# Output projections and mix of a two-layer block as three fp32r passes, with a share of the elementwise work on GpSimd

## The reference, cut to what matters

```python
y_a = nsa_attention(...) @ w_attn_o[l]          # (512, 512) @ (512, 1024)
y_b = spatial_gating(...) @ w_sgu_o[l]          # (512, 256) @ (256, 1024)
y_c = s5_layer(...) @ w_s5_o[l]                 # (512, 256) @ (256, 1024)
g_a, g_b, g_c = jnp.split(jax.nn.sigmoid(branch_g), 3, axis=-1)
merged = g_a * y_a + g_b * y_b + g_c * y_c
x = x + merged @ w_mix_o[l]                     # (512, 1024) @ (1024, 1024)
h = rms_norm(x, norm_ffn_g[l])
x = x + hierarchical_moe(h, ...)                # 32 experts, 6.3 MB of weights each
```

## Time and profile before

| | |
|---|---|
| median of 3 runs | 1970.93 us (1968.88 to 1974.15) |
| the profiled execution, its own time | 1967.01 us |
| its span in the trace | 1965.3 us |
| mean granted clock of TensorE | 0.989 |
| PE busy | 1899.9 us (97%) |
| DVE, ACT, POOL busy | 945.9, 431.4, 99.4 us |

### The profile page before, as it was taken

How to read it: one execution, slowest core, us unless ns; L and a number is a source line. 1 busy time by engine, 2 the same in 40 slices (tenths; PEclk the granted TensorE clock), 3 DMA queues, 4 the chain that set the end, 5 groups by cost and what they waited for, 6 DMA issues and landing times. The chain is left out here.

```text
span 1965.3 us, 26006 instructions
## 1 busy us (share of the span) xinstructions
PE 1899.9 (97%) x10104; PEld 1122.1 (57%) x10105; DVE 945.9 (48%) x1875; ACT 431.4 (22%) x816; POOL 99.4 (5%) x205
## 2 busy tenths in 40 slices
PE   6999999999999999999899999999999999999995
PEld 4868777645554454454357877775465455455442
DVE  7754555345443443443478455553363343343344
ACT  4413444102211111111233244440121111111112
POOL 4500000000000000000063000000000000000000
PEclk9999999999999999999999999999999999999998
DMA  4222112333699999999722221132528999999993
GB/s 165 65 92 86 65 63 67 129 107 157 266 425 426 425 429 426 425 426 426 321 70 65 92 73 68 54 105 89 216 91 338 426 427 423 428 430 422 423 428 156
DMA packets 56398, 482.10 MB, mean 245 GB/s; under 512 B 9584, under 2 KB 22384, under 8 KB 27376
## 3 DMA queue, kind: packets, MB, share of 16 engines
q1 hardware_dynamic: 56304, 480.80, 60.4%
HBM read 476.59 MB, written 4.19 MB: 245 GB/s over the span
## 5 line engine op out<-in xcount | busy, mean ns | idle before, releaser
L1756 DVE TENSOR_TENSOR x_tokens<-x_tokens,ps 128x512 f32<-128x512 f32 x240 | 161.7, 687 | 236.9 <-PE ps L990 236.0
L1056 PE MATMUL ps<-arena,branch 128*64 128x512 f32 x512 | 226.6, 595 | 0.0
L1056 PE MATMUL ps<-slabs,branch 128*64 128x512 f32 x512 | 226.6, 595 | 0.0
L1006 PE MATMUL ps<-slabs,arena 128*64 128x512 f32 x512 | 225.0, 592 | 0.7 <-issue 0.7
L1006 PE MATMUL ps<-arena 128*64 128x512 f32 x512 | 225.0, 592 | 0.1
L1007 PE MATMUL ps<-arena 128*64 128x512 f32 x512 | 225.1, 592 | 0.0
L1007 PE MATMUL ps<-slabs,arena 128*64 128x512 f32 x512 | 225.0, 592 | 0.0
L749 PE MATMUL ps<-h_hi,w_parts 128*128 128x512 f32 x768 | 210.8, 408 | 1.5 <-DVE w_parts L1411 1.5
L749 PEld LDWEIGHTS ps<-h_hi,w_parts 128*128 128x128 f32 x768 | 135.1, 189 | 38.8 <-issue 9.2
L1006 PEld LDWEIGHTS ps<-slabs,arena 128*64 128x64 f32 x512 | 70.1, 137 | 146.0 <-issue 145.9
L1006 PEld LDWEIGHTS ps<-arena 128*64 128x64 f32 x512 | 70.0, 137 | 144.8 <-issue 144.8
(11 more groups left out here) (346 smaller groups left out, 2972.5 us busy)
## 6 DMA issues: line engine op xcount, KB each, us to landing
arena<-in_expert_w_gate SPq DMA_DIRECT2D x32, 2048.0 KB, 12.4
arena<-in_expert_w_up SPq DMA_DIRECT2D x32, 2048.0 KB, 16.8
arena<-in_expert_w_down SPq DMA_DIRECT2D x32, 2048.0 KB, 9.8
slabs<-in_expert_w_gate SPq DMA_DIRECT2D x32, 2048.0 KB, 15.4
slabs<-in_expert_w_up SPq DMA_DIRECT2D x32, 2048.0 KB, 19.9
slabs<-in_expert_w_down SPq DMA_DIRECT2D x32, 2048.0 KB, 14.1
slabs<-in_gate_w SPq DMA_DIRECT2D x24, 1024.0 KB, 4.8
slabs<-in_dense SPq DMA_DIRECT2D x10, 2048.0 KB, 8.1
```

What stands on the lines that cost most here:

```text
L1006: nc.tensor.matmul(ps[0:64, BANK_GU[b], :], xk, low[:, k, :], start=(k == 0), stop=(k == ND - 1), tile_position=(0, 0))
L1056: done = nc.tensor.matmul(ps[64 * b:64 * b + 64, BANK_Y[half], :], hidT[:, k, CAP * b:CAP * (b + 1)], w_down[b][:, k, half * 512:(half + 1 ...
L1756: v.tensor_tensor(xs, xs, ps[:, BANK_BACK[n % 2], :], ALU.add).then_inc(s["back_added"], 1)
```

## The change

The output projections and the mix become three fp32r passes. The three branch outputs, the merged rows and the four kinds of weights are each split in a high and a low part. The two weight slabs of the output projections become four half slabs (k = 20 to 23), the two of the mix four (k = 24 to 26, and a fourth, here called 27, that goes to the gates' place). PE makes 24 separate products p (`OUT_PRODUCTS`: branches 1, 2, 0 for columns 0 to 3, then for 4 to 7) into six rotating banks; DVE merges each by one instruction (`outp_free`), GpSimd adds the first two branches (`sum_two`), and DVE adds the third. The low parts of the mix weights are made by GpSimd as well. Of the first expert weights only one slab is loaded at `merge_done` 8 instead of four. The core of the diff:

```diff
-N_SLAB = 24
+N_SLAB = 28
-S_KS, S_V, S_CMP, S_GATE, S_ATT, S_SGU, S_MIX = 3, 6, 7, 8, 20, 21, 22
+S_KS, S_V, S_CMP, S_GATE, S_OUT, S_MIX = 3, 6, 7, 8, 20, 24
+OUT_PRODUCTS = [(br, 4 * half + n) for half in range(2) for br in (1, 2, 0) for n in range(4)]
+MIX_SLABS = ((S_MIX, S_MIX + 1), (S_MIX + 2, S_MIX + 3))
+MIX_SPLIT = (S_MIX, S_MIX + 3, S_MIX + 1, S_MIX + 2)
...
-                            10: (s["hidden_done"], 2), S_MIX + 1: (s["outp_done"], ND)}
+                            10: (s["hidden_done"], 2), S_OUT + 3: (s["outp_done"], 8), S_MIX: (s["outp_done"], 12),
+                            S_MIX + 1: (s["outp_done"], 20), S_MIX + 2: (s["outp_done"], 24)}
...
+                            if k == S_MIX:
+                                sp.wait_ge(s["outp_free"], 16)
+                                sp.dma_start(view(O_GATE + SLAB, SLAB // 2), io["dense"][layer, 8][:, 2048:4096]).then_inc(s["mix4_in"], 16)
...
                     sp.wait_ge(s["merge_done"], ND)
-                    load_gate_up(sp, 0, 0)
+                    sp.dma_start(w_place[0][0], expert_rows(io["expert_w_gate"], 0, ND)).then_inc(w_in_sem[0][0], 16)
+                    sp.wait_ge(s["proj_done"], J_END - 1)
+                    load_gate_up(sp, 1, 1)
+                    sp.wait_ge(s["proj_done"], J_END)
+                    sp.dma_start(w_place[0][1], expert_rows(io["expert_w_up"], 0, ND)).then_inc(w_in_sem[0][1], 16)
                     load_down(sp, 0, 0)
...
+                        if p >= 6:
+                            pe.wait_ge(s["outp_free"], p - 5)
+                        for part, (wp, hp) in enumerate(((w[0], br_hi[br]), (w[1], br_hi[br]), (w[0], br_lo[br]))):
...
+                    def mix(t, half, upper, begin, end):
...
+                        if t == 0:
+                            pe.wait_ge(s["w_hi_ready"], S_OUT + 3 + MIX_SPLIT.index(k))
+                            pe.wait_ge(s["w_lo_pool"], LO_PIECES * (MIX_SPLIT.index(k) + 1))
+                        for j in range(4):
+                            if t == 0 and half == 0:
+                                pe.wait_ge(s["m_lo_ready"], 4 * upper + j + 1)
+                            for part, (mp, wp) in enumerate(((m_hi, 0), (m_hi, 1), (m_lo, 0))):
...
+                    for k in range(2):
+                        for t in range(2):
+                            mix_half(t, 0, k)
...
+                    for n in range(4):
+                        merged_hi(n)
+                    split_hi(S_MIX)
+                    act.wait_ge(s["mix4_in"], 16)
+                    nc.scalar.activation(mix4_hi, view(O_GATE + SLAB, SLAB // 2), ACT.Identity).then_inc(s["w_hi_ready"], 1)
+                    merged_hi(4)
+                    merged_hi(5)
+                    split_hi(S_MIX + 1)
...
+                        v.scalar_tensor_tensor(to, g, 1.0, ps[:, 2 + p % 6, :], ALU.add, ALU.mult).then_inc(s["outp_free"], 1)
+                        if br == 0:
+                            dve.wait_ge(s["outp_free"], p + 1)
+                            dve.wait_ge(s["two_summed"], n + 1)
+                            v.tensor_tensor(gates[:, 2 * ND + n, :], merged[:, n, :], g, ALU.add).then_inc(s["merge_done"], 1)
...
+                    def merged_lo(n):
+                        dve.wait_ge(s["m_hi_ready"], n + 1)
...
+                        v.tensor_tensor(m_lo[:, n, :], raw, m_hi[:, n, :], ALU.subtract).then_inc(s["m_lo_ready"], 1)
...
+                    def sum_two(n):
...
+                        pool.wait_ge(s["outp_free"], OUT_PRODUCTS.index((2, n)) + 1)
+                        g.tensor_tensor(merged[:, n, :], merged[:, n, :], gates[:, 2 * ND + n, :], ALU.add).then_inc(s["two_summed"], 1)
...
+                    for n_ in range(4):
+                        sum_two(n_)
+                    for i, k in enumerate(MIX_SPLIT):
+                        if i == 1:
+                            for n_ in range(4, ND):
+                                sum_two(n_)
+                        pool.wait_ge(s["w_hi_ready"], S_OUT + 3 + i)
...
+                        for piece in range(LO_PIECES):
...
+                            g.tensor_tensor(lo[:, part], raw[:, part], hi[:, part], ALU.subtract).then_inc(s["w_lo_pool"], 1)
```

More of the change, by code:

```diff
@@ new lines, in _ @@
+                    mix_parts = {k: [u[k % 3].rearrange("p (k c) -> p k c", k=4) for u in (w_hi, w_lo)] for k in range(S_MIX, S_MIX + 3)}
+                    mix_parts[S_MIX + 3] = [u.rearrange("p (k c) -> p k c", k=4) for u in (mix4_hi, mix4_lo)]
+                    mix_out = {}
+                    def mix(t, half, upper, begin, end):
+                        if begin:
+                            mix_out[t, half] = bank_p(J_MIX + MIX_JOBS.index((t, half)))
+                        k = MIX_SLABS[half][upper]
+                        if t == 0:
[4 more added lines that the diff above has]
+                                pe.wait_ge(s["m_lo_ready"], 4 * upper + j + 1)
+                            at = slice(t * P, (t + 1) * P)
+                            for part, (mp, wp) in enumerate(((m_hi, 0), (m_hi, 1), (m_lo, 0))):
+                                last = nc.tensor.matmul(mix_out[t, half], mp[:, 4 * upper + j, at], mix_parts[k][wp][:, j, :],
+                                                        start=(begin and j == 0 and part == 0), stop=(end and j == 3 and part == 2))
+                        if end:
+                            last.then_inc(s["proj_done"], 1)
@@ L890, in turn_h2, with mix_half @@
+                    def mix_half(t, half, k):
+                        first = 0 if half == 0 else 1
+                        mix(t, half, first if k == 0 else 1 - first, k == 0, k == 1)
+                    for k in range(2):
+                        for t in range(2):
+                            mix_half(t, 0, k)
                     def turn_h2(t):
@@ new lines, in _ @@
+                    split_lo(LO_PIECES)
+                    for p in range(8, 12):
+                        merge(p)
+                        if p > 8:
+                            merged_lo(p - 9)
+                    split_lo(LO_PIECES)
+                    merged_lo(3)
+                    for p in range(12, 20):
+                        merge(p)
+                    for p in range(20, 24):
+                        merge(p)
+                        if p > 20:
+                            merged_lo(p - 17)
@@ L1636, in add_mix @@
+                    merged_lo(7)
                     def add_mix(t, half):
```

198 lines of the change are left out of this document (119 added, 79 removed).

## The result

The changed kernel takes 1937.9 us (median of 4 runs, 1936.2 to 1940.5), the kernel before 1971.2 (4 runs on the same chip); the ratio is 0.983, 95% interval 0.981 to 0.985. The forecast was 1938. The profiled execution took 1937.5 us with a span of 1935.7.

A forecast was written before the change was run, and what follows sets the result against it. The prediction took PE, busy 97% of the span, as the bound. Its terms, 22.7 - 3.1 - 1.7 - 1.3 = 16.6 us a layer, 33 in all, gave 1970.9 - 33 = 1938 us, range 1930 to 1946.

The forecast's parts named there:

- TensorE's passes: Output projections and mix: 384 fp32r passes at 0.227 us replace 256 fp32 records at 0.429, saving 22.7 us a layer.
- The start at nothing: Start of output projections: splitting first slab and branch in attention's gaps costs nothing; without that cover 2.5 us.
- GpSimd, stall 3.1 us: Mix: PE waits 3.1 us a layer for GpSimd's 16 instructions up to slab 25's last piece; bounds 0 and 7.2.
- Merges do not collide: DVE merges, reading PSUM and one SBUF operand, don't contend with GpSimd; otherwise the stall would be 7.2 us.
- Clock after the stall: Behind PE's new wait in the mix, a lower granted clock costs 1.7 us a layer; bounds 0 and 3.4.
- Routing: Before the rank of tile 2, PE waits 1.3 us a layer because 12 passes cover only 2.7 us of routing.
- Expert weights hidden: First expert product: its second slab, now queued behind two others, lands in time with 8 us to spare.
- A: Rival in the mix: GpSimd keeps up, no stall or clock loss, 21.4 us a layer gained, 1928 us; chance 0.19.
- D: Rival: GpSimd's sixteen instructions alone make the kernel slower, gain gone at 2.6 us each, 1991 at 3.2; chance 0.04.
- B: Rival in the mix: GpSimd slower, stall 7.2 us, gain 11.2 a layer, 1949 us, or 1953; chance 0.14.
- C: Rival at the first expert: weights come late, PE stands still 5 us a layer, 1948 us; chance 0.04.
- E: Rival in the expert loop: transfers filling the queue eat the gain, no change, 1971 us; chance 0.04.

The follow-up runs named there:

- e_double: Changed kernel with a second instruction, its output unread, ahead of each of GpSimd's 16 weight pieces per layer; 1970.2 us, ratio 0.999 to 1.001.
- e_order: Changed kernel with GpSimd and ScalarE taking slab 25 before slab 27; 1930.9 us, ratio 0.979 to 0.981.
- c_after: The changed kernel measured again without any edit; 1939.5 us, ratio 0.982 to 0.986.
- e_inter: Changed kernel with GpSimd's pieces interleaved (two of slab 27, slab 25, rest of 27, slab 26) and ScalarE's splits reordered; 1931.0 us, ratio 0.978 to 0.981.
- e_sum_dve: Changed kernel with the sum of the first two branches moved from GpSimd back to VectorE; 1935.4 us, ratio 0.981 to 0.985.

## Why the prediction was right, step by step

- **TensorE's passes** (22.7 us saved). Right in kind, 1.9 too much. 192 passes of the output projections took 417.15 - 372.92 = 44.23 us, 0.230 each, and a quarter of the mix 2.80 for twelve, 0.233. I took 0.227 and kept 0.235 as a bound. A product of twelve passes steps 2.72 us (411.70 to 414.42 in its rows), one of six 1.40: the short ones cost 0.04 us more at their head. Together 89.0 us, so 20.8 saved.
- **The start at nothing**: right. TensorE's wait before its last products of attention is 0.69 us as it was, and no other stands in front of the first output product.
- **VectorE no time**: right; no wait for a bank in the profile.
- **GpSimd, stall 3.1 us**: measured 3.09 (3.06 in layer 1). Of its parts: pieces began 29.4 us into the stage (forecast 29.1), the 16 instructions took 23.7 us (forecast 22.9), and TensorE was there after 50.0 us (forecast 49.0). The instruction is dearer than the 1.18 taken, 1.27 at four clear of VectorE's double readers; what I had as 8 meetings of 0.50 shows, for example, as 1.72 in place of 1.27 for each of the four of slab 27. The row ended 1.1 us later in the stage than forecast, and TensorE came 1.0 us later: that the two cancel is luck; that the wait is this row's end, e_double shows. The prediction's own figures give 423.5 - 420.5 = 3.0 and a bound of 427.5 - 420.5 = 7.0, where it wrote 3.1 and 7.2. And slab 25, which it had landing at 409, landed at 413.1 in e_order; in the changed kernel that is covered, since GpSimd takes it only at 419.6.
- **Merges do not collide**: the first reading was right, 0.61 us each beside GpSimd. The Trainium skill (SBUF — State Buffer, Who interferes with whom) says that a VectorE instruction with at most one SBUF input, outside the two-port modes, does not contend with GpSimd, and that one with two SBUF inputs does. The trace agrees with both: 0.61 us for a merge, up to 1.78 for a low part. The same section of the Trainium skill calls this contention "an exclusive lock"; measured here, a piece of slab 27 took 1.72 us, somewhat less than a piece and a low part one after the other (1.27 + 0.62).
- **Clock after the stall** (1.7): 0 in the first profile, 1.4 and 1.6 in the second. A term of 1.7 was too high in all four: their mean is 0.75. Before the change the last gather of the stage ran at the lower level (granted clock 0.58 from 502.5 to 506.1) and took 3.49 us up to the first expert product at 506.07; in the first profile after it is 489.79 - 487.16 = 2.63, a new wait of 0.46 included. That gave back 0.9 us that no term of mine had.
- **Routing** (1.3): measured 0.87. TensorE was released by the last instruction but one of the routing (L1806), and its twelve passes covered 3.0 us and not 2.7.
- **Expert weights hidden**: right. The first product waits 0.46 us, for VectorE and not for a transfer.
- **Sum**: 20.8 - 3.1 - 0.9 + 0.9 = 17.7 us, which is the measured stretch of the first profile; forecast 16.6. The mechanism was right, but part of the nearness is luck: 1.9 us too much for the passes stands against 1.7 of clock that was not lost, 0.4 of routing and 0.9 at the last gather. In c_after the stretch is 1.4 and 2.6 us longer. That the median meets 1938 to 0.1 us is luck as well, since what lies outside the two stages moved by 5.8 us between the profiled executions.
- **Rivals.** A (no stall) needed only another order: e_inter is A, at 1931 where I had priced it at 1928; its stretches are 19.5 and 19.6 us shorter than before, where A had 21.4, chiefly since the passes gave 1.9 less. D is e_double's slope. B, C and E didn't happen: from the first expert product of layer 0 to the first product behind the expert loop (L359, now L372) it is 473.0 us before and 473.2 after. The warning of the Trainium skill (Perfetto Trace Analysis, Optimizing Scalar/DVE Operations) that moving work between VectorE and GpSimd "might not help" fits e_sum_dve: with the sums on VectorE the kernel is no slower (1935.4 us against 1937.9 and 1939.5).

## What to carry to other kernels

When TensorE gets faster by a trick that needs prepared operands, lay out the preparing engine's row, instruction by instruction, against the moment each operand is wanted: here the gain was right to 1.1 us a layer in the first profile, and the only new wait above 1 us was for an operand from that row. Then order that row by when its inputs land and when its outputs are wanted, and let no ready work stand behind work whose transfer is still under way; e_order and e_inter took the wait from 3.1 us to 1.6 and to 0.3 or less, and the time down by 0.4% both times, though part of that is the clock and not the wait. A difference of 1 to 3 us between two profiles can be the clock at another place, so compare the parts (the wait, the passes behind it, the rest) and not only the medians, which here hid the gain of e_inter over e_order.

## What was unexpected in the hardware

- The clock's lower level moves about. The same kernel in two executions: 24 passes behind the same 3.1 us wait in 5.83 us (1.00) and in 7.27 (0.79). The last gather, behind waits of 1.7 and 0.4 us, took 3.5 us up to the first expert product in both layers before the change, 2.6 in both layers of the first profile after it, and one of each in c_after. The start of layer 1 was granted 0.86 on the mean in both profiles of the changed kernel, 0.93 before.
- The wait of TensorE behind the barrier between the layers is 3.6 to 3.7 us in eight of the twelve profiles, 4.5 in one and 7.2 to 7.3 in three, with the same work just before and behind it. No run here shows why.
- A GpSimd subtraction of 128x512 takes 1.25 to 1.27 us (two inputs from SBUF) and about 1.7 beside VectorE instructions of two SBUF inputs, which themselves go from 0.62 to between 1.07 and 1.78: a meeting costs VectorE 0.5 to 1.2 us and GpSimd about 0.5.
